# A decoder layer with routed experts: rows gathered by GpSimd from a table by token, with a list of tokens by place made on chip, in place of rows scattered to their places

## The reference, cut to what matters

```python
def grouped_moe(u, w_router, w1, w3, w2):
    xt = u.reshape(B * T, D)
    aff = jax.nn.softmax((xt @ w_router).astype(jnp.float32), axis=-1)
    group_score = lax.top_k(aff.reshape(-1, N_GROUPS, EXPERTS_PER_GROUP), TOP_K)[0].sum(-1)
    g_sel = jnp.argmax(group_score, axis=-1)
    ...
    top_w, top_i = lax.top_k(jnp.where(in_group, aff, -1.0), TOP_K)
    top_w = top_w / jnp.sum(top_w, axis=-1, keepdims=True)
    ...
    for e in range(N_EXPERTS):
        h = jax.nn.silu(xt @ w1[e]) * (xt @ w3[e])
        y = y + gate[:, e:e + 1] * (h @ w2[e])
```

## Time and profile before

| | |
|---|---|
| median of 3 runs | 689.77 us |
| the profiled execution | 687.71 us |
| its span | 686.0 us |
| TensorE matmul busy | 605.6 us (88%) |
| VectorE busy | 400.6 us (58%) |
| ScalarE, GpSimd busy | 157.6 and 71.2 us |
| DMA read, written | 156.74 MB, 22.81 MB |
| SP's, GpSimd's, ACT's queue, share of 16 engines | 62.1%, 5.5%, 3.7% |

### The profile page before, as it was taken

The page is one execution under the profiler, slowest core; times in us unless marked ns, Lnnn a source line. Parts: engine busy times, 40 slices in busy tenths (PEclk is TensorE's granted clock), DMA queues, the critical chain, the costliest instruction groups (busy, mean ns, idle before and its releaser), DMA issues.

```text
span 686.0 us, 15994 instructions
## 1 busy us (share of the span) xinstructions
PE 605.6 (88%) x6493; PEld 378.1 (55%) x6493; DVE 400.6 (58%) x1018; ACT 157.6 (23%) x405; POOL 71.2 (10%) x121
## 2 busy tenths in 40 slices
PE   0999999998898899779999989999999789999940
PEld 0654474577666566555447646666655445656620
DVE  4746709324489999962335645666655544666636
ACT  5201000103566667851335000000000000000000
POOL 6010000008100000000000400000000000000022
PEclk9999999999899999999999989999999989999975
DMA  8995936144699400019403899999999999999828
GB/s 312 389 400 210 358 117 245 62 126 132 204 332 216 140 1 1 1 57 427 193 32 149 342 360 387 390 387 379 380 380 391 391 406 399 376 370 383 302 62 330
DMA packets 43973, 180.39 MB, mean 263 GB/s; under 512 B 5714, under 2 KB 22698, under 8 KB 35722
## 3 DMA queue, kind: packets, MB, share of 16 engines
q1 hardware_dynamic: 35328, 157.11, 62.1%
q0 software_dynamic: 4352, 13.91, 5.5%
q10 hardware_dynamic: 4236, 8.55, 3.7%
HBM read 156.74 MB, written 22.81 MB: 262 GB/s over the span
## 4 chain that ended last, share of the span: by engine, by line
PE 36%; DMA 17%; DVE 1%; POOL 1%; issue 1%; POOLq 0%; DVEq 0%; ACT 0%
DMA pool_sb<-in_moe_w 14%; PE score L1766 13%; PE score L1632 8%; PE score L1777 8%; PE bank L1756 2%; PE bank L1386 1%; DMA pool_sb<-expert_rows,idx 1%; DMA pool_sb<-expert_rows 1%; POOL pool_sb L855 1%; PE bank L1734 1%; PE bank L1670 1%; DVE gate_row L1308 0%; PE bank L1681 0%; DMA expert_rows<-gate_row 0%; PE bank L1577 0%
## 5 line engine op out<-in xcount | busy, mean ns | idle before, releaser
L1766 PE MATMUL score<-pool_sb 128*32 128x256 f32 x2688 | 157.8, 388 | 10.8 <-DMA pool_sb<-in_moe_w 8.4
L1766 PEld LDWEIGHTS score<-pool_sb 128*32 128x32 f32 x2688 | 89.0, 112 | 72.5 <-issue 14.7
L1411 PE MATMUL bank<-pool_sb 128*128 128x512 f32 (+2 forms) x256 | 84.6, 491 | 0.7 <-DVE pool_sb L932 0.5
L1777 PE MATMUL score<-pool_sb 128*32 128x256 f32 x1312 | 81.0, 388 | 1.7 <-DMA pool_sb<-in_moe_w 1.4
L730 ACT ACTIVATE pool_sb<-score 128x128 f32<-128x128 f32 x41 | 11.4, 278 | 259.7 <-PE score L1766 250.0
L1308 DVE TENSOR_TENSOR gate_row<-score,gate_part 32x256 f32<-32x256 f32 x164 | 67.9, 414 | 3.7 <-PE score L1777 1.4
L1411 PEld LDWEIGHTS bank<-pool_sb 128*128 128x128 f32 x256 | 48.5, 190 | 36.1 <-issue 31.6
L1315 DVE TENSOR_TENSOR pool_sb<-pool_sb,score 128x128 f32<-128x128 f32 x42 | 15.9, 378 | 88.2 <-ACT pool_sb L730 86.4
L1632 PE MATMUL score<-pool_sb 128*128 128x512 f32 (+1 forms) x144 | 57.1, 549 | 0.0
L1777 PEld LDWEIGHTS score<-pool_sb 128*32 128x32 f32 x1312 | 39.1, 111 | 25.5 <-DMA pool_sb<-in_moe_w 2.0
L636 ACT ACTIVATE pool_sb<-pool_sb,nmax 128x128 f32<-128x128 f32 (+2 forms) x96 | 50.0, 526 | 4.6 <-DVE nmax L1036 4.5
(11 more groups left out here) (274 smaller groups left out, 692.1 us busy)
## 6 DMA issues: line engine op xcount, KB each, us to landing
pool_sb<-in_moe_w SPq DMA_DIRECT2D x48, 2048.0 KB, 30.6
pool_sb<-in_ada_w SPq DMA_DIRECT2D x16, 1024.0 KB, 7.0
expert_rows<-zeros_f SPq DMA_DIRECT2D x17, 512.0 KB, 6.3
expert_rows<-gate_row POOLq DMA_DIRECT2D x42, 128.0 KB, 7.0
pool_sb<-expert_rows ACTq DMA_DIRECT2D x41, 128.0 KB, 6.9
pool_sb<-in_ada_w SPq DMA_DIRECT2D x8, 640.0 KB, 12.6
pool_sb<-in_w_out SPq DMA_DIRECT2D x4, 1024.0 KB, 16.5
pool_sb<-in_ada_w SPq DMA_DIRECT2D x8, 384.0 KB, 8.6
```

What stands on the lines that cost most here:

```text
L1411: m = nc.tensor.matmul(pj_bank(g, i)[:, 0:n], featT[:, k, i * P:(i + 1) * P], w_stage[:, g % 3, k, 0:n], start=(k == 0), stop=(k == KD - 1))
L1766: mm = nc.tensor.matmul(banks[0][h * BT:(h + 1) * BT, 0:2 * HB], xgT[:, k, :], w[:, :, h, :], start=(k == 0), stop=(k == KD - 1))
L1777: mm = nc.tensor.matmul(y[h * BT:(h + 1) * BT, 0:DN], h_of[:, c * BT:(c + 1) * BT], exp_w2[e % 3][:, c, h * DN:(h + 1) * DN], start=(c == ...
```

## The change

No scatter is made. `x_hat`'s rows go to a table in DRAM by token, `xh_dram` (four plain stores of 512 KB, three by SP and the last by ACT). Each row of it is also four parts of 1 KB (`xh_parts`). On chip a list is made: entry (p, b) is the index of the 1 KB part that belongs on partition p of block b. It is a sum of outer products, 32 matmuls of `rows_hot` (row in the block times the token's number, 128x32) with `blocks_hot` (the block, 128x67), one for each of eight token groups and four column parts; VectorE adds the part's number and casts (`row_list`). For each block from the third on, GpSimd copies one column of the list, waits for it, runs a small operation and issues an indirect gather of 128 pieces of 1 KB straight into `xg_in`, which now is 128 partitions by 256; the gather of block g+5 stands ahead of the store of block g in its loop. All blocks are transposed as two 128x128 pieces, as the first two were. Expert 3's matrices and expert 2's w1 have new waits. Routing's arrays have a tensor of their own. The block counts are made after the list. The zeroing of `xs` stays (16 stores, waited for by VectorE ahead of the routing).

```diff
-N_ROWS = -(-(MAXB + 2) * BT // P) * P
+N_ROWS = MAXB * BT
+N_LIST = MAXB + 3
...
-        xg = rowbuf[0:BT, 0:D]
-        xg_in = [rowbuf[(1 + n) * BT:(2 + n) * BT, 0:D] for n in range(2)]
+        xg = rowbuf[:, 0:DN]
+        xg_in = [rowbuf[:, (1 + n) * DN:(2 + n) * DN] for n in range(2)]
...
+        xh_dram = nc.dram_tensor("normalised_rows", (T, D), F32, kind="Internal").ap()
+        xh_tiles = xh_dram.rearrange("(i p) d -> p i d", p=P)
+        xh_parts = xh_dram.rearrange("t (c n) -> (t c) n", c=NT)
...
+            def store_x_hat(queue, i):
+                queue.wait_ge(r_xh, i + 1)
+                queue.dma_start(xh_tiles[:, i, :], norm_x[:, i, :]).then_inc(s_xh, 16)
+
             for i in range(TT - 1):
                 store_x2(i)
+                store_x_hat(sp, i)
             sp.wait_ge(o_pj, NS)
             load_matrix(1, 0)
+            store_x2(TT - 1)
             load_matrix(1, 1)
-            store_x2(TT - 1)
-            sp.wait_ge(s_scat, 16 * N_SCAT)
+            sp.wait_ge(o_x, NS)
+            sp.wait_ge(r_lt, TT + 1)
+            load_matrix(3, 0)
             sp.wait_ge(r_xh, TT)
             sp.wait_ge(r_tr, NS)
             sp.wait_ge(s_keep, 16 * TT)
             load_matrix(3, 1)
-            sp.wait_ge(m_ye, 1)
-            load_matrix(3, 0)
-            sp.wait_ge(s_scat, 16 * N_SCAT)
-            sp.wait_ge(s_scat_end, 16 * (2 * TT - N_SCAT))
-            sp.wait_ge(r_prod, 4)
+            sp.wait_ge(s_xh, 16 * TT)
+            sp.wait_ge(r_prod, 5)
             load_matrix(2, 0)
...
-            def xg_load(g, n):
-                act.dma_start(xg_in[n], xs[bass.ds(g * BT, BT), :]).then_inc(s_xg[n], 16)
+            act.wait_ge(r_xh, TT)
+            act.dma_start(xh_tiles[:, TT - 1, :], norm_x[:, TT - 1, :]).then_inc(s_xh, 16)
 
             def silu_of(g):
                 act.wait_ge(m_h1, g + 1)
                 nc.scalar.activation(silu, banks[0][:, 0:HB], ACT.Silu).then_inc(m_si, 1)
 
-            def block_of_rows(g, n):
-                silu_of(g)
-                act.wait_ge(m_cp, g + 3)
-                xg_load(g + 4, n)
-
             for g in range(2):
                 silu_of(g)
-            act.wait_ge(s_scat, 16 * N_SCAT)
-            act.wait_ge(s_scat_end, 16 * (2 * TT - N_SCAT))
-            xg_load(3, 1)
-            xg_load(4, 0)
-            act.wait_ge(m_cp, 4)
-            xg_load(5, 1)
             act.wait_ge(t_gs, 1)
             pairs = block_pairs(act)
             last = act.value_load(block_start[0:1, NE + 2:NE + 3], min_val=MIN_BLOCKS * NE - 1, max_val=MAXB)
             with act.Fori(1, pairs - 1) as m:
                 for n in range(2):
-                    block_of_rows(m * 2 + n, n)
+                    silu_of(m * 2 + n)
...
-            pool.wait_ge(s_rows, 16 * N_ZERO)
-            pool.wait_ge(r_xh, TT)
-            for n in range(2 * TT):
-                if n % TT == 0:
-                    pool.wait_ge(t_idx, n // TT + 1)
-                pool.indirect_dma_start(out=xs, out_offset=bass.IndirectOffsetOnAxis(ap=idx[:, n:n + 1], axis=0),
-                                        in_=norm_x[:, n % TT, :], in_offset=None).then_inc(s_scat if n < N_SCAT else s_scat_end, 16)
-
+            def gather_rows(g, n):
+                nc.gpsimd.tensor_copy(rows_now[:, n:n + 1], row_list[:, bass.ds(g, 1)]).then_inc(r_now, 1)
+                pool.wait_ge(r_now, g - NH + 1)
+                nc.gpsimd.tensor_tensor(scr[:, 0:TT], ones[:, 0:TT], ones[:, 0:TT], ALU.mult)
+                pool.indirect_dma_start(out=xg_in[n], out_offset=None, in_=xh_parts,
+                                        in_offset=bass.IndirectOffsetOnAxis(ap=rows_now[:, n:n + 1], axis=0)).then_inc(s_xg[n], 16)
+
+            pool.wait_ge(s_xh, 16 * TT)
+            pool.wait_ge(r_hot, 3)
+            for g in range(NH, NH + 2):
+                gather_rows(g, g % 2)
             pool.wait_ge(t_gs, 1)
             pairs = block_pairs(pool)
...
+                    pool.wait_ge(m_cp, m * 2 + n + 4)
+                    gather_rows(m * 2 + n + 5, 1 - n)
                     store_rows(y_sb[n], m * 2 + n, n)
...
-            nc.vector.tensor_copy(idx[:], posf).then_inc(t_idx, 2)
-            dve.wait_ge(s_rows, 16 * N_ZERO)
+            dve.wait_ge(r_lt, TT + 1)
...
-            pairs = gsf[:, NE + 1:NE + 2]
-            ch(nc.vector.tensor_scalar(pairs, gsf[:, NE:NE + 1], 0.5, 0.25, ALU.mult, ALU.add))
-            ch(nc.vector.tensor_scalar(pairs, pairs, ROUND, None, ALU.add))
-            ch(nc.vector.tensor_scalar(pairs, pairs, -ROUND, None, ALU.add))
-            nc.vector.tensor_scalar(gsf[:, NE:NE + 1], pairs, 2.0, None, ALU.mult)
-            ch(nc.vector.tensor_scalar(gsf[:, NE + 2:NE + 3], pairs, 2.0, -1.0, ALU.mult, ALU.add))
-            nc.vector.tensor_copy(block_start[:], gsf[0:1, :]).then_inc(t_gs, 1)
+            ch(nc.vector.tensor_scalar(block_at[:], posf, 1.0 / BT, 0.5 / BT - 0.5, ALU.mult, ALU.add))
+            ch(nc.vector.tensor_scalar(block_at[:], block_at[:], ROUND, None, ALU.add))
+            ch(nc.vector.tensor_scalar(block_at[:], block_at[:], -ROUND, None, ALU.add))
+            ch(nc.vector.scalar_tensor_tensor(out=row_at[:], in0=block_at[:], scalar=-float(BT), in1=posf, op0=ALU.mult, op1=ALU.add))
+            ch(nc.vector.tensor_tensor(rows_hot[:], place[:, 0:BT].unsqueeze(1).broadcast_to([P, 2 * TT, BT]),
+                                       row_at[:].unsqueeze(2).broadcast_to([P, 2 * TT, BT]), ALU.is_equal))
+            nc.vector.tensor_tensor(rows_hot[:], rows_hot[:], token[:].unsqueeze(2).broadcast_to([P, 2 * TT, BT]), ALU.mult).then_inc(r_hot, 1)
 
             def first_rows(g):
-                dve.wait_ge(r_prod, g + 2)
-                if g < 2:
-                    if g > 0:
-                        dve.wait_ge(m_xt, g)
-                    m = nc.vector.tensor_copy(first_xg, banks[5 + g][:, 0:DN])
-                else:
-                    for c in range(NT):
-                        m = nc.vector.tensor_copy(xg[:, c * DN:(c + 1) * DN], banks[5 + g][c * BT:(c + 1) * BT, 0:DN])
-                m.then_inc(m_cp, 1)
+                dve.wait_ge(r_prod, g + 2 if g < 2 else g + 3)
+                if g > 0:
+                    dve.wait_ge(m_xt, g)
+                nc.vector.tensor_copy(xg, banks[5 + g][:, 0:DN]).then_inc(m_cp, 1)
...
+            nc.vector.tensor_tensor(blocks_hot[:], place[:, 0:N_LIST].unsqueeze(1).broadcast_to([P, 2 * TT, N_LIST]),
+                                    block_at[:].unsqueeze(2).broadcast_to([P, 2 * TT, N_LIST]), ALU.is_equal).then_inc(r_hot, 1)
             xg_T(0)
+            dve.wait_ge(r_prod, 4)
+            ch(nc.vector.tensor_scalar(listf[:], banks[3][:, 0:N_LIST], part[:], None, ALU.add))
+            nc.vector.tensor_copy(row_list[:], listf[:]).then_inc(r_hot, 1)
...
-            def first_T():
+            def xg_T():
                 for q in range(2):
-                    m = nc.tensor.transpose(banks[4][:, q * P:(q + 1) * P], first_xg[:, q * P:(q + 1) * P], ident[:])
+                    m = nc.tensor.transpose(banks[4][:, q * P:(q + 1) * P], xg[:, q * P:(q + 1) * P], ident[:])
                 m.then_inc(m_xt, 1)
 
             for i in range(TT):
                 pe.wait_ge(r_pick, i + 1)
                 m = pick_rows(0, i)
             m.then_inc(r_prod, 1)
-            pick_rows(1, 0)
             pe.wait_ge(m_cp, 1)
-            first_T()
-            for i in range(1, TT):
+            xg_T()
+            for i in range(TT):
                 m = pick_rows(1, i)
             m.then_inc(r_prod, 1)
-
-            def xg_T():
-                for k in range(KD):
-                    m = nc.tensor.transpose(banks[4][:, k * BT:(k + 1) * BT], xg[:, k * P:(k + 1) * P], ident[0:BT, 0:BT])
-                m.then_inc(m_xt, 1)
+            pe.wait_ge(r_hot, 2)
+            for n in range(2 * TT):
+                for k in range(NT):
+                    m = nc.tensor.matmul(banks[3][k * BT:(k + 1) * BT, 0:N_LIST], rows_hot[:, n, :], blocks_hot[:, n, :],
+                                         start=(n == 0), stop=(n == 2 * TT - 1))
+            m.then_inc(r_prod, 1)
 
             def inner(e, g):
```

80 lines of the change are left out of this document (48 added, 32 removed).

## The result

The changed kernel takes 662.64 us (median of 4 runs, 662.40 to 665.58) against 690.57 for the kernel before (median of 4): ratio 0.960 [0.955, 0.966], 28 us faster. The forecast was 710, slower than before, with a range from 677 to 724. The profiled execution took 662.40 us (span 660.8) against 687.71.

The account below looks back on a forecast made before the run. TensorE at 5.92 us a block and a saturated weight stream were taken to bound the kernel neck and neck; 397 + 207 + 74 = 678 against 657 made it 21 us slower, 710 us, range 677 to 724.

Parts of the forecast that it names:

- A gather has eight data packets and a completion on each engine: six turns more, 7.0 + 6 x 0.68 = 11.1 us.: Loop: each 1 KB piece waits its turn behind a 16 KB weight packet, so gathers land late; 7.4 us a block.
- the 9.1 from which the rivals decide: Loop: a gather landing in under 9.1 us is hidden, the point from which the packed-pieces case decides.
- the first rival: Loop: GpSimd's queue packs several 1 KB pieces into a turn, gather as quick as old load; -10 us, chance 0.27.
- From 397 us on ... 304 turns of 0.68: 207 us.: Loop: the remaining 38 weight matrices, 8 packets on each engine, take 207 us to stream.
- The framed rival: Loop: 1 KB pieces packed into shared turns, TensorE keeps 5.7 us a block; 678 to 680 us, chance 0.27.
- The sum's form: Loop: 28 blocks at 7.4 us while weights stream, 13 at 5.7 after, ending at 678 instead of 657.
- Transposes, 0.24 us a block: Each block: eight 32-row transposes (0.61 us) become two of 128 rows (0.37), saving 0.24 us.
- Stall and clock at the loop's start, 5.9 us: Loop start: TensorE's wait for block 3's rows and the fallen clock after it go, saving 5.9 us.
- List and picks, 1.4 us: Ahead of the loop: 32 list matmuls add 0.9 us, second block's picks no longer running ahead 0.5.
- Earlier weights, 8 us: Before the loop: plain stores replace the scatter, expert 3's weights go out before routing ends; stream gains 8 us.
- GpSimd 2.0 us from the release to the gather's start: Each block: copy, wait and dummy operation on GpSimd take 2.0 us before the gather starts.
- Zero-cost steps: Ahead of the loop: one-hots hidden on VectorE, later block counts and stores of normalised rows cost nothing.

Follow-up runs that it names:

- e8: Changed kernel with two first blocks made by TensorE instead of three, gather of block g+4 (not g+5) ahead of block g's store: 668.14 us, ratio 0.964.
- e12: Changed kernel with finished rows scattered from 128 partitions, two first blocks instead of three, block g+5's gather ahead of block g's store: 662.95 us, ratio 0.964.
- e9: Kernel before, block rows loaded as plain transfer of 128 pieces of 1 KB on GpSimd's queue onto 128 partitions, two transposes a block: 723.13 us, ratio 1.047.
- e2: Kernel before, block rows loaded on ACT's queue as 128 pieces of 1 KB onto 128 partitions, two transposes a block: 754.70 us, ratio 1.095.
- e6: Changed kernel with the gather as 64 pieces of 2 KB onto partitions 64 to 127 and four transposes: 678.02 us, ratio 0.983.
- e7: Changed kernel with the gather as 64 pieces of 2 KB onto partitions 32 to 95 and four transposes: 662.91 us, ratio 0.960.
- e5: Changed kernel with each block's pair of transposes made twice: 665.06 us, ratio 0.965.
- e4: Changed kernel with expert 3's weights requested only when the third block is picked, as late as before: 664.44 us, ratio 0.967.
- e1: Kernel before with the block loads, still 32 pieces of 4 KB, moved from ACT's to GpSimd's queue: 685.79 us, ratio 1.001.
- e10: Changed kernel with finished rows kept on 128 partitions and stored by indirect transfer of 128 pieces of 1 KB: 661.35 us, ratio 0.956.

## Why the prediction was wrong, step by step

- **"A gather has eight data packets and a completion on each engine: six turns more, 7.0 + 6 x 0.68 = 11.1 us."** This is the step that failed, and with it the sign: 28 us faster where 21 slower was forecast. The gather has two data packets and a completion on each engine, like the old load, and is over in time for every copy; where it is on the chain (e8, e12) it takes 6.8 to 8.9 us, under the 9.1 from which the rivals decide. The rule under it held where packets really were small: e9, with the forecast's nine turns for a load and twelve for a block, lost 32 us, and e2, with 32 turns on four engines, 69. What failed is that a rule read from ACT's queue and plain transfers was carried over to an indirect transfer on another queue, for which no row stood. The Trainium skill's packet of up to about 4096 bytes (DMA: Bandwidth & Descriptors, "SWDGE vs HWDGE vs iDMA"), named beside the first rival, is what the trace shows for the gather; it had 0.27.
- **"From 397 us on ... 304 turns of 0.68: 207 us."** This term was mis-sized in two ways. It leaves out the blocks' own loads and stores, which go through the same engines: 38 matrices are 79.7 MB and 42 loads and stores 11.0 MB more, at 384 GB/s 236 us and not 207, and the kernel before still moved 376 GB/s between 640 and 645 us. And the pace was taken as a property of the weights, where it was partly that of the block loads, which landed on half of the ports. In the changed kernel the rate is 408 GB/s from 610 to 615 us and 136 from 620 to 625, so the stream ends near 617: 220 us after 397, and 90.7 MB at 421 GB/s are 215. The framed rival took over the old pace, which is why it gave 678 to 680 and not 663; e6, a gather without extra packets that lands on half of the ports, took 678.0, and the landing place is worth the other 15 us (e7).
- **The sum's form.** With 5.69 us for every block it is 397 + 41 x 5.69 = 630 whatever the stream takes, and TensorE ended at 632.4. That tests the block's length, and says nothing of the stream.
- **Transposes, 0.24 us a block:** 5.69 for 5.92 is measured. What that was worth depends on what else limits: adding as much back in the fast stream cost 2.4 to 3.9 us of 9 (e5).
- **Stall and clock at the loop's start, 5.9 us:** gone as forecast, clock 1.00 from 400 to 430 us.
- **List and picks, 1.4 us:** the list matmuls take 0.95 on the chain (0.9 was taken), and inner group 0 stops 0.43 us before its last eighth. Right.
- **Earlier weights, 8 us:** e4 gives 2 by the medians, 5 by the ratios. Taken too high, if the medians are right: with a stream that keeps up, most of an early start is given back.
- **GpSimd 2.0 us from the release to the gather's start:** 1.0. Too high, without effect, since GpSimd had 2.3 us of slack a block.
- **Zero-cost steps** (one-hots on VectorE, block counts after the list, stores of the normalised rows): no wait on them appears on TensorE in the loop. Of the 25.2 us between the two profiled spans, 2.7 lie ahead of the routing. There before's granted clock was 0.93 from 150 to 175 us and 0.90 from 175 to 210, and 1.00 in the changed kernel; e1, whose code there is before's, has 1.00 in both, so this is put down to the one execution, not to the change.

## What to carry to other kernels

Count turns, not bytes, when small transfers share the DMA engines with large ones, but first get the packet count of just that kind of transfer on just that queue, and its completions, which tell on how many engines it runs. And look where a small, frequent load lands in SBUF: on partitions 32 to 63, 64 to 95 or 64 to 127 it held a large stream beside it 8% down, while 32 to 95 and all 128 did not, and the shift or the spread cost nothing. Before pricing a saving on one engine, ask whether a second limit stands right beneath it.

## What the runs showed of the hardware

- The landing place of 128 KB every 5.7 us changed the rate of all that went by meanwhile from 388 to 423 GB/s (e6, e7), at a DMA share of 1.01 in both: the share does not tell a packet that moves from one that is held up. The rows of 16 KB beside a landing took 0.84 us instead of 0.62 (e6); stores that read 32 partitions held up none (before, e10).
- 128 pieces of 1 KB onto 128 partitions made 32 packets of 4 KB as an indirect transfer (after, e10's stores), 128 packets of 1 KB and 4 completions instead of 16 on ACT's queue (e2), and 32 of 4 KB with some 98 tiny ones as a plain transfer on GpSimd's queue (e9); the times were 663, 755 and 723 us.
- A gather that stands behind a store in GpSimd's program waits with it: one block less of lead made a chain of 12.2 us for two blocks, on average, out of a hidden path (e8).
- A stop of 3.6 us on TensorE was followed by 3 us at a granted clock of 0.50, and cost 1.7 us on top of the wait (after, 545 us).
